# The gated product of the paired feed-forward units is turned by VectorE instead of TensorE, and products, additions and rounding move to later steps

## What is computed

```
D_MODEL = 2048; SEQ = 256; DEPTH = 2; D_FF = 5632

def swiglu_ffn(h, w_gate_up, w_down):
    gu = h @ w_gate_up
    gate, up = gu[..., :D_FF], gu[..., D_FF:]
    return (jax.nn.silu(gate) * up) @ w_down

# in each layer, after attention:
h = rmsnorm(x, g[2])
y = swiglu_ffn(h, ffn_w_gate_up[i], ffn_w_down[i])
x = x + rmsnorm(y, g[3])
```

## Time and profile before

| | us |
|---|---|
| median of 3 runs | 2077.8 (2077.33 to 2078.42) |
| the profiled execution | 2077.3 |
| its span | 2075.6 |
| TensorE busy | 2059.2 (99%) |
| VectorE busy | 1676.9 (81%) |
| ScalarE busy | 1263.0 (61%) |
| GpSimd busy | 354.4 (17%) |

### The profile page before, as it was taken

One profiled execution on the slowest core, in us unless ns is written; L12 is line 12 of the kernel. 1 busy time (PEld: TensorE's weight loads), 2 busy tenths in 40 slices (PEclk: granted clock), 3 DMA queues, 4 the chain that ended last, 5 costly groups with the idle time before them and its releaser, 6 DMA issues.

```text
span 2075.6 us, 31330 instructions
## 1 busy us (share of the span) xinstructions
PE 2059.2 (99%) x9523; PEld 1687.3 (81%) x9523; DVE 1676.9 (81%) x2859; ACT 1263.0 (61%) x2081; POOL 354.4 (17%) x479
## 2 busy tenths in 40 slices
PE   9999999999999999999999999999999999999998
PEld 7877887888888888887888887888888888888886
DVE  6798568887888888779898898568888788778877
ACT  7776566655666556656666556566556656556653
POOL 2110001111111111110152342001111111111110
PEclk9999999999999999999999999999999999999999
DMA  7699879899998899886686786869899888999984
GB/s 262 208 253 255 221 234 266 225 266 266 234 253 233 241 267 262 239 244 197 205 249 215 213 252 212 256 206 256 239 269 263 238 244 224 265 267 232 254 227 156
DMA packets 255632, 496.56 MB, mean 239 GB/s; under 512 B 17856, under 2 KB 27488, under 8 KB 254256
## 3 DMA queue, kind: packets, MB, share of 16 engines
q1 hardware_dynamic: 203648, 381.47, 56.9%
q0 software_dynamic: 51600, 113.59, 27.8%
q10 hardware_dynamic: 288, 0.33, 0.1%
HBM read 476.41 MB, written 18.91 MB: 239 GB/s over the span
## 4 chain that ended last, share of the span: by engine, by line
PE 93%; DVE 3%; DMA 1%; issue 1%; ACT 1%; POOL 0%; SPq 0%; POOLq 0%; DVEq 0%; ACTq 0%
PE bank L1671 30%; PE bank L1673 29%; PE bank L1672 29%; PE bank L1718 1%; PE bank L1743 1%; DVE ring_lo L1038 1%; PE bank L1781 1%; DMA x_scratch<-x_sb 1%; PE bank L1684 0%; DMA stage<-ffn_w_gate_up 0%; DVE h_t L1386 0%; DVE ring_lo L1036 0%; PE bank L1701 0%; DVE ring_lo L1046 0%; DMA stage<-ffn_w_down 0%
## 5 line engine op out<-in xcount | busy, mean ns | idle before, releaser
L1671 PE MATMUL bank<-ring_hi,a_hi 128*128 128x512 f32 x2240 | 881.3, 393 | 2.0 <-DVE ring_lo L1038 1.3
L1673 PE MATMUL bank<-ring_hi,a_lo 128*128 128x512 f32 x2240 | 872.5, 390 | 0.0
L1672 PE MATMUL bank<-ring_lo,a_hi 128*128 128x512 f32 x2240 | 871.9, 389 | 0.0
L1038 DVE SCALAR_TENSOR_TENSOR ring_lo<-stage,g_t,ring_hi 128x512 fp32r<-128x512 f32 x992 | 716.0, 756 | 97.9 <-ACT ring_hi L791 97.0
L791 ACT ACTIVATE ring_hi<-stage,g_t 128x512 fp32r<-128x512 f32 x992 | 660.6, 712 | 153.0 <-DMA stage<-ffn_w_gate_up 87.9
L803 ACT ACTIVATE ring_hi<-down_w 128x1024 fp32r<-128x1024 f32 x280 | 296.8, 1060 | 386.9 <-PE bank L1673 348.5
L1671 PEld LDWEIGHTS bank<-ring_hi,a_hi 128*128 128x128 f32 x2240 | 420.5, 188 | 94.8 <-issue 5.7
L1673 PEld LDWEIGHTS bank<-ring_hi,a_lo 128*128 128x128 f32 x2240 | 420.4, 188 | 88.6
L1672 PEld LDWEIGHTS bank<-ring_lo,a_hi 128*128 128x128 f32 x2240 | 420.8, 188 | 84.4
L1595 POOL DMA_DIRECT2D down_w<-ffn_w_down x160 | 192.8, 1258 | 1093.5 <-DVE ring_lo L1046 1093.5
L1046 DVE TENSOR_TENSOR ring_lo<-down_w,ring_hi 128x1024 fp32r<-128x1024 f32 x280 | 340.5, 1219 | 41.4 <-ACT ring_hi L803 40.6
(11 more groups left out here) (173 smaller groups left out, 1405.3 us busy)
## 6 DMA issues: line engine op xcount, KB each, us to landing
stage<-ffn_w_gate_up SPq DMA_DIRECT2D x352, 512.0 KB, 6.1
down_w<-ffn_w_down POOLq DMA_DIRECT2D x160, 512.0 KB, 7.8
down_w<-ffn_w_down SPq DMA_DIRECT2D x120, 512.0 KB, 7.5
stage<-fox_w_in SPq DMA_DIRECT2D x96, 512.0 KB, 4.7
stage<-swa_w_in SPq DMA_DIRECT2D x48, 512.0 KB, 4.7
stage<-swa_w_out SPq DMA_DIRECT2D x64, 256.0 KB, 5.7
stage<-fox_w_out SPq DMA_DIRECT2D x32, 512.0 KB, 5.5
stage<-ffn_w_down SPq DMA_DIRECT2D x16, 512.0 KB, 5.1
```

Source lines behind the costliest of these rows:

```text
L1038: nc.vector.scalar_tensor_tensor(out=lo, in0=src, scalar=g_t[:, row * KT + j:row * KT + j + 1], in1=hi, op0=ALU.mult, op1=ALU.subtract).th ...
L1671: nc.tensor.matmul(dst, hi_a, hi_w, start=start, stop=False, skip_group_check=goes_on)
L1672: nc.tensor.matmul(dst, hi_a, lo_w, start=False, stop=False, skip_group_check=goes_on)
L1673: return nc.tensor.matmul(dst, lo_a, hi_w, start=False, stop=stop, skip_group_check=goes_on)
```

## The change

The eight transposes of TensorE at step 4 of each gate unit are removed, and with them the copy `h_first` and a wait of the up unit for the sums. VectorE turns `h_sb` into `h_t` in SBUF with sixteen 32-partition transposes of 256 elements (`turn_group`), four at each of the steps 2, 3, 4 and 7 of the gate unit. ScalarE rounds all of `h_t` in one instruction at step 10, where it was two at steps 6 and 7; VectorE makes the rest and the sums at step 11, and the sums are rounded at 13 and 15 (before 10 and 12). The first six products of the gate unit stand at steps 22 to 31 where they stood at 18 to 29, the additions at 24 to 31 with the sixth at step 1 of the up unit, the rounding of T2, T3, T4 and of the next unit's B11 and B21 two or three steps later, and that of the up unit's B22 at its own step 1 instead of step 31 of the gate unit. The up unit's own tables stay otherwise.

```diff
-PRODUCT_STEPS = ({18: 0, 20: 1, 22: 2, 24: 3, 26: 4, 29: 5}, {8: 0, 11: 1, 14: 2, 21: 3, 23: 4, 26: 5})
+PRODUCT_STEPS = ({22: 0, 23: 1, 25: 2, 27: 3, 29: 4, 31: 5}, {8: 0, 11: 1, 14: 2, 21: 3, 23: 4, 26: 5})
...
-PAIR_HI = ({5: (0, T1), 20: (0, T2), 22: (0, T3), 28: (0, T4), 24: (1, B11), 26: (1, B21), 31: (1, B22)},
+PAIR_HI = ({5: (0, T1), 23: (0, T2), 24: (0, T3), 26: (1, B11), 28: (1, B21), 31: (0, T4)},
...
+HIDDEN_SPLIT = 10
+S_HI_STEPS = {13: 0, 15: 1}
+TURNED_STEPS = {2: 0, 3: 1, 4: 2, 7: 3}
...
-                nc.scalar.activation(h_hi[:, :, tok(t)], main[2 + t][:, :].rearrange("p (k m) -> p k m", k=4), ACT.Identity).then_inc(ht_hi, 1)
+                nc.scalar.activation(h_hi[:, :, :], h_t[:, :, :], ACT.Identity).then_inc(ht_hi, 1)
...
+            def turn_group(u, i, a):
 
                 layer, g, _ = ffn_part(u)
-                dve.wait_ge(ht_hi, hidden_split(layer, g - 1, t) + 4 * i)
-                nc.vector.tensor_tensor(h_lo[:, :, tok(t)], main[2 + t][:, :].rearrange("p (k m) -> p k m", k=4),
-                                        h_hi[:, :, tok(t)].bitcast(F32), ALU.subtract).then_inc(ht_lo, 1)
+                if a == 0:
+                    dve.wait_ge(hidden, 2 * (layer * FG + g - 1) + 2 + 4 * i)
+                for b in range(P // Q):
+                    src = h_sb[Q * a:Q * (a + 1), :, :].rearrange("p t (k b j) -> p t k b j", k=4, j=Q)[:, :, :, b, :]
+                    dst = h_t[Q * b:Q * (b + 1), :, :].rearrange("p k (t a i) -> p t k a i", t=NT, i=Q)[:, :, :, a, :]
+                    last = nc.vector.transpose(dst, src)
+                if a == P // Q - 1:
+                    last.then_inc(h_turned, 1)
...
-                        if pair_unit(u) and ffn[2] == 0 and s == TURNED_STEP:
-                            for t in range(NT):
-                                hidden_transposes(ffn[0] * FG + ffn[1] - 1, i, t, main[2 + t], h_turned)
```

More of the change, by code:

```diff
@@ L657, in hidden_split @@
         def hidden_split(layer, g, t):
-            return layer * 2 * FG + 2 * g + t + 1
+            return layer * (GW + 2) + g + 1 + (t if g == GW else 0)
         def wait_swept(eng, u, i, t, n=0):
@@ L961, in unit @@
                                                  scale=pre_r[:, t:t + 1]).then_inc(gate_read, 1)
[L962 to L963 removed]
+                        if pair_unit(u) and part == 0 and s == HIDDEN_SPLIT:
+                            hidden_heads(u, i)
                         if pair_unit(u) and part == 0 and s in S_HI_STEPS:
@@ L1358, in unit @@
                                 sum_rests(u, i, S_HI_STEPS[s - 1])
+                        if pair_unit(u - 1) and part == 1 and s == 1:
+                            add_pair(u - 1, i, NPROD - 2)
                         if pair_unit(u - 1) and s == LAST_ADDED:
@@ L1776, in down_pair, with hidden_transposes @@
                 last.then_inc(pair_done, 1)
-            def hidden_transposes(f, i, t, to, signal):
-                pe.wait_ge(hidden, 2 * f + t + 1 + 4 * i)
+            def hidden_transposes(f, t):
+                pe.wait_ge(hidden, 2 * f + t + 1)
                 for k in range(4):
-                    last = nc.tensor.transpose(to[:, k * P:(k + 1) * P], h_sb[:, t, k * P:(k + 1) * P], ident[:, :])
-                last.then_inc(signal, 1)
+                    last = nc.tensor.transpose(xt_ps[t][:, k * P:(k + 1) * P], h_sb[:, t, k * P:(k + 1) * P], ident[:, :])
+                last.then_inc(ht_last, 1)
             def forget_gate():
@@ L1844, in accumulator @@
                             pe.wait_ge((gate_read, hidden)[part], 2 * (f - 1) + t + 1 + 4 * i)
-                            if part == 1:
-                                pe.wait_ge(s_made, 4 * (layer * GW + g) + 8 * i)
                         elif part == 0:
```

42 lines of the change are left out of this document (17 added, 25 removed).

## The result

The change makes the kernel **slower: 2148.5 us** (median of 4 runs, 2147.07 to 2150.22) against 2077.6 (4 runs beside them), ratio 1.0343 with a 95% interval of 1.0325 to 1.0361. That is 71 us more where 2125 us (47 more) was forecast with a range of 2085 to 2152. The profiled execution took 2147.1 us with a span of 2145.0.

The account below looks back on a forecast made before the run. TensorE, busy 99% of the span, was taken as the bound; without its transposes and waits 2057.0 us. VectorE's stalls made it +43 us over 20 groups and +4.5 for first groups against 2077.3: 2125 us, range 2085 to 2152.

Parts of the forecast that it names:

- The gain: TensorE loses its transposes, 17.6 us over 20 groups, and its waits for `h_sb` at first groups, 2.7 us: 2057.0 us.
- Load: Sixteen VectorE transposes a group at 0.45 us each: 7.2 us more, 59.3 us of work in a group of 62.6.
- The walk: VectorE's row followed through gate and up unit against TensorE's due times; it found three stalls in a group.
- First stall: Gate unit's fifth product waits for the third addition, done at +28.1 but due at +27.2: 0.9 us a group.
- third: Stall at the up unit's T2 product: 1.5 us, plus 0.2 for a longer transfer, 1.7 us a group.
- Second stall: T4's product waits for the sixth addition, done at +35.4 but due at +34.9: 0.4 us a group.
- first groups and others: Each layer's first group starts VectorE 3.6 us later; two such groups, less 2.7 us of waits that go: +4.5 us.
- What was costed at nothing: Other moves: later silu, GpSimd's DMA order, SyncE's later loads, `h_first` and the accumulator wait gone; nothing or little.
- (a): Rival: VectorE fits, the walk is off by 1.3 us or more at every deadline, all stalls go: 2057 us; chance 0.11.
- (b): Rival: up unit's T2 transfer takes 9 us or less, only the gate unit's 1.3 us remain: 2090 us; chance 0.14.
- (c): Rival: transposes cost 0.52 us each, 2147 us, or also hold up GpSimd's T2 DMA, 2161 us; chance 0.10.

Follow-up runs that it names:

- e_copy: The kernel after the change with its sixteen transposes a group replaced by four 128x256 copies, steps and waits kept: 2059.8 us, ratio 0.992.
- e_up_late: The kernel after with three products of the up unit, their additions and the roundings of T4 and the next B22 two steps later: 2139.3 us, ratio 1.0301.
- e_pe_late: The kernel before, still transposing on TensorE, with the later steps for products, additions and roundings of the kernel after: 2078.3 us, ratio 1.0011.

## Why the prediction was right, and where it fell short

- **The gain, 17.6 + 2.7 us: right.** e_copy came to 2059.8 where this alone gives 2057.
- **Load: right.** 0.45 a transpose from start to start (1.78, 3.58 and 1.80 for four, eight and four). The 311 ns that the prediction took from the Trainium skill (VectorE: DVE Perf Modes) stand there, in the section "The three transpose paths", for 128x128 turned only within its 32x32 blocks, which is not the turning that this kernel needs; so the 2.5 us worked out from them were no price for it, and the sum did not use them.
- **The walk: right to 0.2 us in the gate unit, where T4's chain is left aside, and 0.35 early at T1's rest in the up unit.** With the gate unit's start at 443.96: T1's rest at +11.0 (+10.9 said), `h_lo` after 1.13 us of idle at +15.2 (+15.1), T1's rest in the up unit at +40.65 (+40.3), T2's product at +55.45 and so 14.8 us after it (14.2 and 0.2 said).
- **First stall 0.9, measured 0.90; third 1.7, measured 1.81** in this group. Over the run the third was smaller than forecast, as the account below shows.
- **Second stall 0.4: the step that failed.** The walk found that T4's transfer, at its median of 7.8 us, makes VectorE 0.5 us late, and left this out of the sum. Measured, the transfer takes 6.9 to 9.2 us at this place (7.8 in the median, 7.9 in mean), and GpSimd issues it at +24.8, 0.3 later than said. So with a transfer of 7.8 the gap is 1.2 us and not 0.4, as in the group of the multiplication at 1710.58 (GpSimd, then TensorE; 1.18 by the starts):

```profile
1732.56 1.19 POOL L1602 DMA_DIRECT2D down_w<-ffn_w_down  x1 [11.05 <-DVE ring_lo L1041]
```

```profile
1744.15 0.47 PE L1678 MATMUL bank<-ring_hi,h_hi 128*128 128x512 f32 x1 [1.01 <-DVE y_sb L1101]
```

  What the transfer takes more or less goes nearly whole into the gap. In the group shown further up it takes 7.2 and the gap is 0.62: GpSimd issues at 468.76, ScalarE rounds at 476.06, VectorE's rest starts at 477.16. In the group of the multiplication at 846.41 ScalarE starts 9.2 us after the issue, and the gap is 2.5 (GpSimd, ScalarE, VectorE, TensorE):

```profile
868.39 1.20 POOL L1602 DMA_DIRECT2D down_w<-ffn_w_down  x1 [11.04 <-DVE ring_lo L1041]
```

```profile
877.63 1.06 ACT L802 ACTIVATE ring_hi<-down_w 128x1024 fp32r<-128x1024 f32 x1 [6.08 <-DMA down_w<-ffn_w_down]
```

```profile
878.72 1.23 DVE L1041 TENSOR_TENSOR ring_lo<-down_w,ring_hi 128x1024 fp32r<-128x1024 f32 x1 [2.17 <-ACT ring_hi L802]
```

```profile
881.35 0.47 PE L1678 MATMUL bank<-ring_hi,h_hi 128*128 128x512 f32 x1 [2.39 <-DVE y_sb L1101]
```

- **The whole run's account.** From the timeline of TensorE through both feed-forward parts of the kernel after, all distances between starts that exceed 0.227 us by more than 0.3, by what ended them, beside what was forecast for 20 groups:

| | forecast, us | measured, us (gaps) |
|---|---|---|
| fifth product, for L1103 | 18 | 16.0 (18) |
| T4's product, for L1101 | 8 | 33.5 (22) |
| up unit's T2, for L1041 | 34 | 20.3 (18) |
| first groups and others | 7 | 6.5 (7) |
| distances wider by 0.03 to 0.3 | 0 | 16.0 (133) |
| together | 67 | 92 |

  In e_copy the same account gives 6.8 us in all, and 92 - 7 is the 87 us between the two kernels but for 2. So the forecast was short by 25 us: 25.5 at T4's products, 16 in slightly wider distances, which stand almost only where stalls are (12 of them in e_copy), and 14 to 16 us back at the other two stalls. That a long second stall covers the third, since TensorE then comes later to T2, fits these sums and e_up_late; it was not tested by itself. Of the 16 us of wider distances 6.7 are 35 matmuls in the four stretches at half clock, which the walk did not have either; the rest are distances wider by about 0.1 us behind the stalls. The 33.5 us at T4's products are 22.7 in 17 gate units (1.34 each where 0.4 was forecast), 9.4 in the three whose T4 follows a taken branch of layer 2's loop (3.1 each), and 1.4 at T4 of the up unit in the last group of each layer.
- **The length of VectorE's row: not foreseen at all.** It is some 8 of these us by the estimate above (the wait at 1676.30 is one for L1101).
- **The clock: not foreseen at all.** Long stalls were followed by stretches at half clock, 7.7 us in the execution profiled. They are why layer 2 lost 67.6 - 66.6 = 1.0 us more in a group than layer 1; three of the four follow the branches of the longer row.
- **What was costed at nothing** (moved steps, order of GpSimd's DMAs) cost about 1 us: e_pe_late. But T4's transfer does take longer at the new steps, 8.1 to 9.8 us in e_copy where it took 5.7 to 7.8 before, and only where there is slack is that hidden.
- **The range.** 2148.5 is inside it by 3.5 us. Its upper part stood for 3.4 us a group; layer 1's groups lost 3.1 and layer 2's 4.1. Direction and mechanism were forecast; that the whole still ended inside with a chain left out, and with the length of the row and the clock not thought of, was luck.
- **Rivals.** (a) needed slack that is there only for the first 3.5 us of load. (b), a quicker transfer, did not come: 14.8 us. (c) named the right size (2147) for a wrong reason: transposes were not dearer, and GpSimd's T2 went out 1.5 us after the start of T1's rest, as before.

## What to carry to other kernels

An engine that is 84% busy can set the end: walk its row against the time at which each piece is wanted, and where a chain has no slack put every part of it into the sum. The half microsecond that was left out here came back in each of the 20 groups. When work moves to another engine, look for the form in which that engine has the least to do: the same turning cost VectorE 7.0 us in sixteen quarter-width instructions and 1.4 in two of full width, once idle engines had done the moving. That alone was not enough: with it the kernel took 2099.8, 2075.0 and 2066.2 us, by the steps at which the rest stood. Count instructions too: in this kernel twelve short ones in a loop cost as much as the eight transposes of TensorE that were to be saved.
